# Two DeltaNet directions in one TensorE stream: the chunk inverse is issued between the state and output products of the step ahead, and the decays of the next step are formed early

## Chip, cores and metric

The kernel runs on one core of a Trainium2 chip. The metric is the device time of one execution in microseconds (us), the median of several runs. Times below are microseconds unless marked ns.

## The reference, cut to what matters

The program computes a two-layer backbone. One of the three branches of each layer is a gated DeltaNet, run forwards and backwards over a context prefix and the latent tokens, four heads of width 128, 512 tokens in all. What the change touches is this recurrence:

```python
decay = jnp.where(incl, jnp.exp(jnp.where(incl, diff, 0.0)), 0.0)
kb = k * beta[..., None]
m = jnp.where(strict, jnp.einsum('bhncd,bhnsd->bhncs', kb, k) * decay, 0.0)
t_inv = lax.linalg.triangular_solve(eye + m, jnp.broadcast_to(eye, m.shape), left_side=True, lower=True)
u = jnp.einsum('bhncs,bhnse->bhnce', t_inv, v * beta[..., None])
w = jnp.einsum('bhncs,bhnsd->bhncd', t_inv, kb * jnp.exp(gam)[..., None])
qk = jnp.einsum('bhncd,bhnsd->bhncs', q, k) * decay

def step(s, xs):
    q_c, k_c, u_c, w_c, qk_c, gam_c = xs
    v_new = u_c - jnp.einsum('bhcd,bhde->bhce', w_c, s)
    o = (jnp.einsum('bhcd,bhde->bhce', q_c * jnp.exp(gam_c)[..., None], s)
         + jnp.einsum('bhcs,bhse->bhce', qk_c, v_new))
    g_last = gam_c[..., -1]
    s = (s * jnp.exp(g_last)[..., None, None]
         + jnp.einsum('bhcd,bhce->bhde', k_c * jnp.exp(g_last[..., None] - gam_c)[..., None], v_new))
    return s, o
```

## The kernel before

The kernel takes chunks of 128 tokens, so each layer has four steps, `j` = 0 to 3. In a step both directions `d` = 0 and 1 work on a tile of tokens each (`ORDER`), with all four heads. Layer 0 writes outputs for all four tiles; the last layer has only two tiles of latent tokens (`nt` = 2), so its steps 0 and 1 write no outputs. All products are fp32 and go through the helper `mm` (L1576), whatever they compute. The order of work on each engine is the order of the code; engines are kept apart by counted semaphores.

A product of four heads, 128x128 by 128x128 each, is called a big group here: four calls, eight instructions in the trace. A product of eight 64x64 blocks (`by_block`) is a small group: eight calls, sixteen instructions in the trace.

A step before the change, on TensorE:

1. Head. `decay`: running sums of the log decay as a matrix, a big group for each direction into bank ONE. `kk` (K times K transposed) into bank TWO. `kq` (keys by queries) into ONE once the decays have been read. VectorE masks the decays (L2086) and ScalarE takes two exponentials of each (L1114 for E, L1115 for the gain EG). VectorE then makes, for one direction after the other, the chain L2095, L2096, L2098, L2100, L2103, L2106: the matrix of the inverse, its first level and its transpose `X`. GpSimd masks the levels (L786).
2. Levels n = 1 to 5 of the inverse, by doubling. For each level: first half of direction 0 and 1 (level times X into TWO), ScalarE copies the result to `Y` (L1127), second half of direction 0 and 1 (XT times Y into ONE), VectorE subtracts (L2114) and transposes (L2118). At the end `beside` and a corner product join the two halves of the 128x128 inverse `T_full`.
3. Tail. `w` (T times decayed keys) and its negated copy on ScalarE (L1142), `fresh` (T times values, and from step 1 on, minus w times state), scaled by beta on VectorE (L2134) into `vnew`, `outs` (state by gained queries from step 1 on, and vnew by scores), `state` (decayed keys by vnew), then the new state on VectorE (L2141, or L2145 from step 1 on). The next step's `decay` waits for the new state, since both use bank ONE.

Banks 0 to 3 hold products of the stages around the DeltaNet and stand free during it. Decayed keys `kg` and `kd` are made on ScalarE by four small scalings each (L1106).

## Time and profile before

| what | value |
|---|---|
| median of 3 runs | 2748.91 us (2747.64 to 2752.01) |
| the profiled execution, its own time | 2748.07 us |
| span of its trace, first to last instruction | 2746.3 us |
| mean granted TensorE clock | 0.963 of full speed |
| the four DeltaNet steps of layer 0 | 149.5 us |
| the four DeltaNet steps of layer 1 | 143.2 us |

The span is the time between the first and the last instruction; the metric has 1.8 us more around it. The two stage times are the sums of four windows each, which are shown below with the busy time of every engine. A busy TensorE is an upper bound on its work, because matmuls overlap and their ends are modelled.

### The profile page before, as it was taken

To read this page: it belongs to the slowest core of one execution; us is meant where nothing else is said; L and a number is where in the kernel's file an instruction comes from. 1 tells how busy PE (TensorE), PEld (TensorE's weight loads), DVE (VectorE), ACT (ScalarE), POOL (GpSimd) and SP (SyncE) were. 2 spreads that over 40 slices of the span, in tenths; PEclk is the share of its full clock that TensorE was granted. 3 is DMA by queue.
4 is the path that set the end of the run, shared out by engine and by line. 5 is a ranking of instruction groups with operands and counts; after the bars stand their busy time and mean duration, and the time that the engine had idled before them with its cause. 6 is when DMAs were issued, how large, how long until landed. Compare 5 with 4: busy or idle time off the path is not lost.

```text
span 2746.3 us, 38445 instructions
## 1 busy us (share of the span) xinstructions
PE 2550.2 (93%) x16316; PEld 2089.2 (76%) x16316; DVE 1346.9 (49%) x2118; ACT 1000.8 (36%) x1551; POOL 80.2 (3%) x108
## 2 busy tenths in 40 slices
PE   3999998989888899989999989999988968889999
PEld 2777776856678777767777768888875758889899
DVE  4323335357776643463332353333355676666654
ACT  2222212355653422232222132322245574344543
POOL 0000000000012100000000000000000002200000
PEclk6999999999989999999999999999999989999999
DMA  5444433201110033324444432222230210034454
GB/s 235 163 175 180 173 138 123 93 31 47 62 47 2 2 132 144 123 75 170 184 165 157 147 139 98 102 92 100 100 108 31 92 62 2 2 133 175 158 183 167
DMA packets 44664, 309.66 MB, mean 113 GB/s; under 512 B 5072, under 2 KB 6224, under 8 KB 7632
## 3 DMA queue, kind: packets, MB, share of 16 engines
q1 hardware_dynamic: 44208, 305.95, 30.3%
q8 instruction: 130, 2.13, 0.3%
q10 hardware_dynamic: 288, 1.27, 0.1%
q14 instruction: 38, 0.31, 0.0%
HBM read 306.15 MB, written 1.05 MB: 112 GB/s over the span
## 4 chain that ended last, share of the span: by engine, by line
PE 85%; DVE 8%; ACT 3%; issue 2%; DMA 1%; SPq 0%; ACTq 0%; DVEq 0%
PE bank L1287 68%; PE bank L1576 7%; PE bank L1303 2%; PE bank L1280 2%; DVE rt L1715 2%; PE bank L1522 1%; PE bank L1500 1%; DVE w_lo L1704 1%; DMA ring<-in_wts 1%; ACT L830 1%; PE bank L1509 1%; ACT w_hi L812 1%; DVE u_lo L1744 1%; DVE sq L1754 0%; DVE work L2103 0%
## 5 line engine op out<-in xcount | busy, mean ns | idle before, releaser
L1704 DVE TENSOR_TENSOR w_lo<-ring,w_hi 128x1024 fp32r<-128x1024 f32 x420 | 510.8, 1224 | 1048.5 <-ACT w_hi L812 1045.5
L1287 PE MATMUL bank<-u_hi,w_hi 128*128 128x512 f32 (+1 forms) x2208 | 817.1, 370 | 84.0 <-DVE w_lo L1704 46.7
L1287 PE MATMUL bank<-u_hi,w_lo 128*128 128x512 f32 (+1 forms) x2208 | 801.6, 363 | 0.0
L1287 PE MATMUL bank<-u_lo,w_hi 128*128 128x512 f32 (+1 forms) x2208 | 799.3, 362 | 0.0
L812 ACT ACTIVATE w_hi<-ring 128x1024 fp32r<-128x1024 f32 x420 | 441.2, 1058 | 965.1 <-PE bank L1287 657.9
L1287 PEld LDWEIGHTS bank<-u_hi,w_hi 128*128 128x128 f32 x2208 | 422.8, 191 | 180.6 <-issue 83.6
L1287 PEld LDWEIGHTS bank<-u_lo,w_hi 128*128 128x128 f32 x2208 | 422.5, 191 | 64.7
L1287 PEld LDWEIGHTS bank<-u_hi,w_lo 128*128 128x128 f32 x2208 | 423.0, 192 | 63.8 <-issue 3.4
L1576 PE MATMUL bank<-work 64*64 64x64 f32 (+1 forms) x3952 | 233.5, 246 | 38.1 <-DVE work L2106 21.4
L1287 PE MATMUL bank<-hidden_hi,w_hi 128*128 128x512 f32 (+1 forms) x704 | 259.8, 369 | 0.0
L1576 PEld LDWEIGHTS bank<-work 64*64 64x64 f32 (+1 forms) x3952 | 220.8, 159 | 50.4 <-POOL work L786 31.8
L1287 PE MATMUL bank<-hidden_hi,w_lo 128*128 128x512 f32 (+1 forms) x704 | 258.5, 367 | 0.0
L1287 PE MATMUL bank<-hidden_lo,w_hi 128*128 128x512 f32 (+1 forms) x704 | 258.5, 367 | 0.0
L1287 PEld LDWEIGHTS bank<-hidden_hi,w_hi 128*128 128x128 f32 x704 | 132.5, 188 | 28.6 <-issue 4.9
L1287 PEld LDWEIGHTS bank<-hidden_lo,w_hi 128*128 128x128 f32 x704 | 132.5, 188 | 24.3
L1287 PEld LDWEIGHTS bank<-hidden_hi,w_lo 128*128 128x128 f32 x704 | 132.5, 188 | 23.7
L1715 DVE RECIPROCAL rt<-rt 128x512 f32<-128x512 f32 (+1 forms) x30 | 92.5, 3082 | 43.1 <-ACT rt L830 43.1
L1303 PE MATMUL bank<-ring,cond 128*32 128x256 f32 x1152 | 82.9, 408 | 21.4 <-DMA ring<-in_wts 21.4
L864 ACT ACTIVATE hidden_hi<-sg 128x512 fp32r<-128x512 f32 (+1 forms) x88 | 50.7, 579 | 127.9 <-DVE sg L1810 127.9
L871 ACT ACTIVATE sg<-bank 128x512 f32<-128x512 f32 (+1 forms) x88 | 46.7, 535 | 116.4 <-PE bank L1287 116.3
L786 POOL TENSOR_TENSOR work<-work,cst 128x256 f32<-128x256 f32 x80 | 67.9, 867 | 417.7 <-DVE work L2098 398.5
L1303 PEld LDWEIGHTS bank<-ring,cond 128*32 128x32 f32 x1152 | 31.4, 114 | 64.0 <-issue 32.1
(195 smaller groups left out, 2407.9 us busy)
## 6 DMA issues: line engine op xcount, KB each, us to landing
ring<-in_wts SPq DMA_DIRECT2D x288, 1024.0 KB, 4.9
h<-in_x SPq DMA_DIRECT2D x8, 256.0 KB, 10.5
par<-in_par ACTq DMA_DIRECT2D x2, 620.0 KB, 6.0
out<-h SPq DMA_DIRECT2D x8, 128.0 KB, 4.1
cst<-in_cst SPq DMA_DIRECT2D x1, 672.0 KB, 10.1
mod_par<-in_mod SPq DMA_DIRECT2D x1, 96.0 KB, 9.7
cond<-in_c SPq DMA_DIRECT2D x1, 8.0 KB, 1.6
```

Of the source, the lines that this page charges most:

```text
L786: pool.tensor_tensor(level[:, d, n % 2, :, :], mt[:, d, :, :], mask, ALU.mult).then_inc(level_ready[d], 1)
L812: act.activation(w_hi[:, b % HALVES, :], half_source(n % RING, part), ACT.Copy).then_inc(weights_rounded, 1)
L830: act.activation(rt[rows, n % 2, 0:w], bank[4 + n % 2][rows, 0:w], ACT.Sqrt, bias=eps[rows, :], scale=1.0 / size).then_inc(roots, 1)
L864: act.activation(h_hi[:, 2 * i + c, 0:w], sg[:, c, 0:w], ACT.Copy).then_inc(hidden_rounded, 1)
L871: act.activation(sg[:, c, 0:w], bank[(q0 + c) % 4][:, 0:w], ACT.Silu).then_inc(drained["a"], 1)
L1280: last = weights.used(pe.matmul(out, lhsT, rhs, start=n == 0, stop=n == len(parts) - 1))
L1287: last = weights.used(pe.matmul(out, lhs[a], rhs[b], start=start and n == 0, stop=stop and n == 2))
L1303: last = pe.matmul(bank[7 - unit % 2][32 * j:32 * j + 32, 0:256], cond32[:, k, :], panel[:, kk, j, :], start=k == 0, stop=k == DC - 1)
L1500: pe.matmul(bank[S_BANKS[a % 4]][:, 0:keys.stop - keys.start], qq[0:QK, hd, t * P:(t + 1) * P], kk[0:QK, hd, keys], start=True, stop=True) ...
L1576: return pe.matmul(out, lhsT, rhs, start=start, stop=stop)
L1704: tt(w_lo[:, b % HALVES, :], half_source(n % RING, part), w_hi[:, b % HALVES, :].bitcast(F32), ALU.subtract).then_inc(panel_left[n % RING] ...
L1715: step(dve.reciprocal(r, r))
```

## The change

Three things change inside the DeltaNet stage.

The algebra: `w` and its negated copy are gone, and so is w times state. In their place `keyed` multiplies the tile's keys by the state (a big group for each direction, steps 1 to 3), and VectorE forms V = values minus decayed `keyed` (`keyed_values`). `fresh` is then a single product T times V, and ScalarE scales it by beta into V in four small scalings (`fresh_values`), where VectorE did it in one operation.

The banks: decays, keys by queries, fresh values and outputs use banks 0 and 2 (FRESH); state and keyed use banks 1 and 3 (STATE). The inverse keeps ONE and TWO.

The order: step j's inverse is issued together with the fresh values, state and outputs of step j-1. `outs` stand in level 1, `key_query` in level 2, `keyed` in level 3, and the decays of step j+1 behind level 5. Gained queries (L2182 of the changed kernel), scores (L2186) and `keyed_values` (L2167) stand behind levels 2, 3 and 4 on VectorE, the new state behind levels 1 and 2. The decayed keys are made on ScalarE behind levels 3 and 4. `beside` has one buffer for both directions, and gained queries go to `rt`.

```diff
-        kg = view(24, 2)
-        blocks = view(26, 5).rearrange("p n (d h c) -> p n d h c", d=2, h=HEADS)
-        mt, beside, X, XT, Y = [blocks[:, n, :, :, :] for n in range(5)]
+        kd = view(24, 2)
+        blocks = view(26, 4).rearrange("p n (d h c) -> p n d h c", d=2, h=HEADS)
+        mt, X, XT, Y = [blocks[:, n, :, :, :] for n in range(4)]
+        V = view(30, 2)
         level = view(32, 2).rearrange("p d (n h c) -> p d n h c", n=2, h=HEADS)
         T_full = view(34, 2)
-        vnew, kd, nwT = E, kg, view(32, 2)
+
+        beside = ada_turned[:, :].rearrange("p (h c) -> p h c", h=HEADS)
+        gain_q = rt
...
+        FRESH, STATE = [bank[0], bank[2]], [bank[1], bank[3]]
...
+                def keep_output(d, j):
+                    t = ORDER[d][j]
+                    if j >= 0 and j % 2 == 0 and t < nt:
+                        act.wait_ge(out_made[d], outs_before(l, j, d) + 1)
+                        act.activation(yb[:, :, t * P:(t + 1) * P], heads(FRESH[d][:, :]), ACT.Copy).then_inc(out_kept[d], 1)
+
+                def decay_keys(d, j):
+                    if j < 3:
+                        act.wait_ge(state_made[d], 3 * l + j)
+                        t = ORDER[d][j]
+                        scaled_heads(kd[:, d, :], ktok[:, t, :], kds[:, d, t, :]).then_inc(kd_ready[d], 1)
+
...
+                def decays(j):
+                    for d in range(2):
+                        act.wait_ge(decay_masked[d], l * 4 + j + 1)
+                        act.activation(E[:, d, :], E[:, d, :], ACT.Exp).then_inc(decay_exp[d], 1)
+                        act.wait_ge(gain_ready[d], l * 4 + j)
+                        act.activation(EG[:, d, :], FRESH[d][:, :], ACT.Exp).then_inc(gain_exp[d], 1)
+
+                def fresh_values(d, j):
+                    act.wait_ge(fresh_made[d], l * 4 + j + 1)
+                    scaled_heads(V[:, d, :], FRESH[d], beta[:, ORDER[d][j], 4 * d:4 * d + 4]).then_inc(fresh_ready[d], 1)
+
+                decays(0)
...
+                    if j:
+                        for d in range(2):
+                            fresh_values(d, j - 1)
...
+                        if n == 1:
+                            for d in range(2):
+                                keep_output(d, j - 1)
+                        if n > 2 and n < 5:
+                            decay_keys(n - 3, j)
...
-                    for d in range(2):
-                        act.wait_ge(w_made[d], it + 1)
-                        act.activation(nwT[:, d, :], TWO[d][:, :], ACT.Copy, scale=-1.0).then_inc(w_kept[d], 1)
...
-
+                        decays(j + 1)
+                for d in range(2):
+                    fresh_values(d, 3)
...
+                def decay(d, j):
+
+                    t = ORDER[d][j]
+                    if j:
+                        pe.wait_ge(kq_read[d], l * 4 + j)
+                    elif d == 0:
+                        wait_drained(pe, (l, "z", 3))
+                    upto = C("upto" if d == 0 else "from")
+                    each(lambda hd, c, _: mm(FRESH[d][:, c], g[:, t, 4 * d + hd:4 * d + hd + 1].to_broadcast([P, P]),
+                                             upto), d, j).then_inc(decay_made[d], 1)
+
+                def fresh(d, j):
+
+                    pe.wait_ge(t_ready[d], l * 4 + j + 1)
+                    pe.wait_ge(kq_read[d], l * 4 + j + 1)
+                    if j < 3:
+                        pe.wait_ge(decay_masked[d], l * 4 + j + 2)
+                        pe.wait_ge(gain_exp[d], l * 4 + j + 2)
+                    if j:
+                        pe.wait_ge(keyed_ready[d], 3 * l + j)
+                    t = ORDER[d][j]
+                    each(lambda hd, c, _: mm(FRESH[d][:, c], T_full[:, d, c], V[:, d, c] if j else vtok[:, t, c]),
+                         d, j).then_inc(fresh_made[d], 1)
+
+                def state(d, j):
+                    pe.wait_ge(fresh_ready[d], l * 4 + j + 1)
+                    pe.wait_ge(kd_ready[d], 3 * l + j + 1)
+                    each(lambda hd, c, _: mm(STATE[d][:, c], kd[:, d, c], V[:, d, c]), d, j).then_inc(state_made[d], 1)
+
+                def outs(d, j):
+                    if ORDER[d][j] < nt:
+                        pe.wait_ge(fresh_ready[d], l * 4 + j + 1)
+                        pe.wait_ge(gain_ready[d], l * 4 + j + 1)
+
+                        def head_out(hd, c, _):
+                            if j:
+                                mm(FRESH[d][:, c], S[:, d, c], gain_q[:, d, c], stop=False)
+                            return mm(FRESH[d][:, c], V[:, d, c], att[:, d, c], start=j == 0)
+                        each(head_out, d, j).then_inc(out_made[d], 1)
+
+                def keyed(d, j):
+
+                    pe.wait_ge(state_ready[d], 3 * l + j)
+                    each(lambda hd, c, t: mm(STATE[d][:, c], kT[:, hd, t], S[:, d, c]), d, j).then_inc(keyed_made[d], 1)
+
+                def key_query(d, j):
+                    if j:
+                        pe.wait_ge(fresh_ready[d], l * 4 + j)
+                        pe.wait_ge(out_kept[d], outs_before(l, j, d))
+                    else:
+                        pe.wait_ge(decay_masked[d], l * 4 + 1)
+                        pe.wait_ge(gain_exp[d], l * 4 + 1)
+                    each(lambda hd, c, t: mm(FRESH[d][:, c], kT[:, hd, t], qT[:, hd, t]), d, j).then_inc(kq_made[d], 1)
+
+                for d in range(2):
+                    decay(d, 0)
...
+                    def beside_level(n, d):
+
+                        if n == 1 and j:
+                            outs(d, j - 1)
+                        elif n == 2:
+                            key_query(d, j)
+                        elif n == 3 and j:
+                            keyed(d, j)
...
+                        if it:
+                            pe.wait_ge(y_kept[d], it * LEVELS)
+                        each(lambda hd, c, t: mm(TWO[d][:, c], kT[:, hd, t], kT[:, hd, t]), d, j).then_inc(kk_made[d], 1)
+                    if j:
+                        for d in range(2):
+                            fresh(d, j - 1)
...
+                            if n == 1 and j:
+                                state(d, j - 1)
+                            first_half(n, d)
+                        beside_level(n, 0)
...
+                            second_half(n, d)
+                        beside_level(n, 1)
+                    if j < 3:
+                        for d in range(2):
+                            decay(d, j + 1)
...
-                    for d in range(2):
-                        pe.wait_ge(kg_ready[d], it + 1)
-                        pe.wait_ge(t_ready[d], it + 1)
-                        each(lambda hd, c, t: mm(TWO[d][:, c], kg[:, d, c], T_full[:, d, c]), d).then_inc(w_made[d], 1)
...
+                for d in range(2):
+                    fresh(d, 3)
+                for d in range(2):
+                    outs(d, 3)
...
+                def new_state(d, j):
+                    dve.wait_ge(state_made[d], 3 * l + j + 1)
+                    dve.wait_ge(out_made[d], outs_before(l, j + 1, d))
+                    if j == 0:
+                        dve.tensor_copy(S[:, d, :], STATE[d][:, :]).then_inc(state_ready[d], 1)
+                    else:
+                        for hd in range(HEADS):
+                            c = slice(hd * P, (hd + 1) * P)
+                            last = stt(S[:, d, c], S[:, d, c], eL[:, d, ORDER[d][j], hd:hd + 1], STATE[d][:, c],
+                                       ALU.mult, ALU.add)
+                        last.then_inc(state_ready[d], 1)
+
+                def keyed_values(d, j):
+                    dve.wait_ge(keyed_made[d], 3 * l + j)
+                    t = ORDER[d][j]
+                    for hd in range(HEADS):
+                        c = slice(hd * P, (hd + 1) * P)
+                        last = stt(V[:, d, c], STATE[d][:, c], egam[:, d, t, hd:hd + 1], vtok[:, t, c], ALU.mult, ALU.add)
+                    last.then_inc(keyed_ready[d], 1)
+
+                def add_output(d, j):
+                    t = ORDER[d][j]
+                    if j % 2 and t < nt:
+                        out = yb[:, :, t * P:(t + 1) * P]
+                        dve.wait_ge(out_made[d], outs_before(l, j, d) + 1)
+                        dve.wait_ge(out_kept[1 - d], outs_before(l, j, 1 - d))
+                        tt(out, out, heads(FRESH[d][:, :]), ALU.add).then_inc(out_kept[d], 1)
+
+                def gained_queries(d, j):
+                    t = ORDER[d][j]
+                    dve.wait_ge(gain_exp[d], l * 4 + j + 1)
+                    dve.wait_ge(out_made[d], outs_before(l, j, d))
+                    tt(heads(gain_q[:, d, :]), heads(EG[:, d, :]), qT[:, :, t * P:(t + 1) * P], ALU.mult).then_inc(gain_ready[d], 1)
+
+                def scores(d, j):
+                    dve.wait_ge(kq_made[d], l * 4 + j + 1)
+                    tt(att[:, d, :], FRESH[d][:, :], E[:, d, :], ALU.mult).then_inc(kq_read[d], 1)
+
+                def decays(j):
+                    for d in range(2):
+                        dve.wait_ge(decay_made[d], l * 4 + j + 1)
+                        for hd in range(HEADS):
+                            c = slice(hd * P, (hd + 1) * P)
+                            last = stt(E[:, d, c], FRESH[d][:, c], gam[:, d, ORDER[d][j], hd:hd + 1],
+                                       C("not_upto" if d == 0 else "not_from"), ALU.subtract, ALU.min)
+                        last.then_inc(decay_masked[d], 1)
+
+                decays(0)
...
+                    if j == 0:
+                        dve.wait_ge(factors_ready, l + 1)
...
+                        if n == 1 and j:
+                            for d in range(2):
+                                add_output(d, j - 1)
+                            new_state(0, j - 1)
+                        elif n == 2:
+                            if j:
+                                new_state(1, j - 1)
+                            for d in range(2):
+                                gained_queries(d, j)
+                        elif n == 3:
+                            for d in range(2):
+                                scores(d, j)
+                        elif n == 4 and j:
+                            for d in range(2):
+                                keyed_values(d, j)
+                    if j < 3:
+                        decays(j + 1)
+                for d in range(2):
+                    add_output(d, 3)
```

TensorE, step 1 of layer 0, before: the rows from its decays to those of step 2. "cst,small" is the decay product; "work 64x64" the inverse, with `beside` and the corners; the 48 behind it are w, fresh, outs and state, and the 16 ahead of it kk and kq.

```order
L1576 MATMUL bank<-cst,small 128x128 x8
L1576 MATMUL bank<-work 128x128 x16
L1576 MATMUL bank<-work 64x64 x192
L1576 MATMUL bank<-work 128x128 x48
L1576 MATMUL bank<-cst,small 128x128 x8
```

TensorE, the same place in the changed kernel: from the decays of step 1, which now stand in step 0, to `keyed` of the first direction in level 3. The row of 20 is kk, fresh of step 0, and its state for direction 0.

```order
L1594 MATMUL bank<-cst,small 128x128 x8
L1594 MATMUL bank<-work,ada_turned 64x64 x8
L1594 MATMUL bank<-work 64x64 x8
L1594 MATMUL bank<-work 128x128 x20
L1594 MATMUL bank<-work 64x64 x8
L1594 MATMUL bank<-work 128x128 x4
L1594 MATMUL bank<-work 64x64 x8
L1594 MATMUL bank<-work 128x128 x4
L1594 MATMUL bank<-work 64x64 x16
L1594 MATMUL bank<-work 128x128 x4
L1594 MATMUL bank<-work 64x64 x16
L1594 MATMUL bank<-work 128x128 x4
```

The inverse was one run of 192 block products; now big groups of four stand between its halves, and no product waits for a new state ahead of kk.

VectorE, the end of step 0 and the head of step 1 before: fresh values, new state, masked decays, then the chain for direction 0.

```order
L2134 TENSOR_TENSOR work<-bank,small 128x512 x2
L2141 COPY work<-bank 128x512 x2
L2086 SCALAR_TENSOR_TENSOR work<-bank,small,cst 128x128 x8
L2095 TENSOR_TENSOR work<-bank,work 64x256 x2
L2096 TENSOR_TENSOR work<-bank,work 64x256
L2098 TENSOR_TENSOR work<-work,small 128x256
L2100 TENSOR_TENSOR work<-work,cst 128x256
L2103 TENSOR_TENSOR work<-cst,work 128x256
L2106 STREAM_TRANSPOSE work<-work 128x256
```

VectorE in levels 1 to 3 of step 1 in the changed kernel: each pair of rows is the subtraction and the transpose of one direction.

```order
L2225 TENSOR_TENSOR work<-work,bank 128x256
L2229 STREAM_TRANSPOSE work<-work 128x256
L2154 COPY work<-bank 128x512
L2225 TENSOR_TENSOR work<-work,bank 128x256
L2229 STREAM_TRANSPOSE work<-work 128x256
L2225 TENSOR_TENSOR work<-work,bank 128x256
L2229 STREAM_TRANSPOSE work<-work 128x256
L2154 COPY work<-bank 128x512
L2182 TENSOR_TENSOR rt<-work 128x512 x2
L2225 TENSOR_TENSOR work<-work,bank 128x256
L2229 STREAM_TRANSPOSE work<-work 128x256
L2225 TENSOR_TENSOR work<-work,bank 128x256
L2229 STREAM_TRANSPOSE work<-work 128x256
L2186 TENSOR_TENSOR work<-bank,work 128x512 x2
```

The copies to the new state, the gained queries (rt) and the scores (128x512 x2 from the bank) moved in between the subtractions, which the next products of the inverse wait for.

## Rows read from the trace of the kernel before

**Rows 1.** The page of the profile: busy engines, and the chain that ended last by line.

```profile
PE 2550.2 (93%) x16316; PEld 2089.2 (76%) x16316; DVE 1346.9 (49%) x2118; ACT 1000.8 (36%) x1551; POOL 80.2 (3%) x108
...
PE bank L1287 68%; PE bank L1576 7%; PE bank L1303 2%; PE bank L1280 2%; DVE rt L1715 2%; PE bank L1522 1%; PE bank L1500 1%; DVE w_lo L1704 1%; DMA ring<-in_wts 1%; ACT L830 1%; PE bank L1509 1%; ACT w_hi L812 1%; DVE u_lo L1744 1%; DVE sq L1754 0%; DVE work L2103 0%
```

**Rows 2.** Busy time in eight steps: window, us, engines' busy (instructions), PEclk, DMA share, GB/s.

```profile
793.70:829.40 35.70, 31.02 (x496) 29.47 (x497) 22.68 (x51) 16.29 (x42) 9.67 (x12) 0.89 0.01 2
829.40:866.70 37.30, 32.60 (x530) 31.09 (x529) 23.80 (x55) 13.38 (x36) 9.72 (x12) 0.95 0.01 2
866.70:906.10 39.40, 33.89 (x530) 32.14 (x530) 24.87 (x60) 14.55 (x38) 9.70 (x12) 0.91 0.01 2
906.10:943.20 37.10, 31.22 (x515) 29.40 (x513) 24.01 (x56) 11.11 (x28) 9.70 (x12) 0.95 0.01 2
2262.30:2297.20 34.90, 30.09 (x480) 28.47 (x481) 22.30 (x51) 15.14 (x40) 9.69 (x12) 0.85 0.01 2
2297.20:2331.40 34.20, 29.39 (x498) 27.57 (x496) 23.79 (x56) 13.38 (x36) 9.72 (x12) 0.95 0.01 2
2331.40:2368.80 37.40, 32.72 (x529) 31.09 (x530) 24.01 (x58) 14.56 (x38) 9.71 (x12) 0.95 0.01 2
2368.80:2405.50 36.70, 30.91 (x514) 29.03 (x512) 24.30 (x56) 11.12 (x28) 9.68 (x12) 0.95 0.01 2
```

**Rows 3.** Timeline of the head of step 1, layer 0: start, us, engine, line, operation.

```profile
829.41 2.10 PE L1576 MATMUL bank<-cst,small 128*128 128x128 f32 x16
...
831.35 3.75 PE L1576 MATMUL bank<-work 128*128 128x128 f32 x32
831.66 0.63 ACT L1114 ACTIVATE work<-work 128x512 f32<-128x512 f32 x1 [2.35 <-DVE work L2086]
832.20 0.58 ACT L1115 ACTIVATE work<-bank 128x512 f32<-128x512 f32 x1
832.59 0.86 DVE L2095 TENSOR_TENSOR work<-bank,work 64x256 f32<-64x256 f32 x2
...
836.14 0.68 PE L1576 MATMUL bank<-work 64*64 64x64 f32 x16 [1.04 <-POOL work L786]
...
838.95 0.45 DVE L2106 STREAM_TRANSPOSE work<-work 128x256 f32<-128x256 f32 x1
839.43 1.29 DVE L2109 TENSOR_TENSOR work<-bank,work 128x512 f32<-128x512 f32 x2
...
839.50 2.79 PE L1576 MATMUL bank<-work 64*64 64x64 f32 x47 [2.68 <-DVE work L2106]
```

**Rows 4.** Timeline of about one level of the inverse in step 0, layer 0, ScalarE and VectorE.

```profile
811.71 0.38 ACT L1127 ACTIVATE work<-bank 128x256 f32<-128x256 f32 x1 [1.37 <-PE bank L1576]
...
812.03 0.99 DVE L2130 TENSOR_TENSOR work<-work 128x512 f32<-128x512 f32 x1
...
812.96 0.42 DVE L2114 TENSOR_TENSOR work<-work,bank 128x256 f32<-128x256 f32 x1
...
813.79 0.38 DVE L2114 TENSOR_TENSOR work<-work,bank 128x256 f32<-128x256 f32 x1
...
814.25 0.39 ACT L1127 ACTIVATE work<-bank 128x256 f32<-128x256 f32 x1 [1.37 <-PE bank L1576]
```

**Rows 5.** Timeline of the end of step 1, layer 0.

```profile
854.15 12.76 PE L1576 MATMUL bank<-work 64*64 64x64 f32 x120 [0.57 <-DVE work L2114]
...
855.97 0.38 ACT L1137 ACTIVATE work<-bank 64x256 f32<-64x256 f32 x1 [0.30 <-PE bank L1576]
...
858.45 2.43 ACT L1106 ACTIVATE work<-work,small 128x128 f32<-128x128 f32 x8
...
866.95 1.12 DVE L2145 SCALAR_TENSOR_TENSOR work<-work,small,bank 128x128 f32<-128x128 f32 x4 [1.56 <-PE bank L1576]
```

**Rows 6.** A window of 2 us where the levels of step 1 begin.

```profile
840.00:842.00 2.00, 2.00 (x43) 2.00 (x41) 1.17 (x4) 0.38 (x1) 1.55 (x3) 0.50 0.04 8
```

**Rows 7.** Window behind the last step of layer 0.

```profile
943.20:1000.00 56.80, 51.90 (x228) 39.52 (x229) 36.06 (x23) 24.19 (x27) 0.00 (x0) 0.94 0.25 95
```

183 lines of the change are left out of this document (48 added, 135 removed).

## The prediction

> **What bounds the kernel now.** I read the page first. TensorE is busy 93% of the span and leads the chain that ended last; L1576, the helper of the DeltaNet, holds 7% of that chain [rows 1]. So the stage is on the path, and only its own length matters. The windows by step give that length: 35.7 + 37.3 + 39.4 + 37.1 = 149.5 us in layer 0 and 34.9 + 34.2 + 37.4 + 36.7 = 143.2 us in layer 1, 292.7 us in all. VectorE is busy 23 to 25 of some 37 us in a step, ScalarE 11 to 16, GpSimd 10 [rows 2].
>
> The timeline then shows three regimes within a step.
>
> Head: 16 decay instructions start at 829.41, kk and kq follow (32 instructions in 3.75 us, so a big group takes 0.94), then TensorE waits 1.04 us, does one small group, and waits 2.68 us more for VectorE's chain of the second direction [rows 3]. The chain is 838.95 + 0.45 - 832.59 = 6.8 us for both directions, 3.4 each. From the first decay to the second direction's first block product: 839.50 - 829.41 = 10.1 us.
>
> Levels: a level repeats every 814.25 - 811.71 = 2.54 us. The reader should see that this is a latency loop: product, copy to Y 0.38, product, subtraction 0.42, with about 0.2 from a product's end to its reader. From the start of the subtraction at 813.79 to that of the copy at 814.25 one small group has ended behind another: 0.46 [rows 4]. Four of them are 1.9 us, so TensorE is short of work for 0.65 us in a level, though the trace calls it busy.
>
> Tail: from 854.15 TensorE runs 120 instructions in 12.76 us without a gap. The last corner is copied at 855.97, so it ended 0.2 earlier, near 855.8; the rest, 96 instructions of w, fresh, outs and state, lasts until 866.7 [rows 2, 5]. There TensorE is the bound.
>
> **The change, part by part.** I lay out one step of the changed kernel with those durations and count from the start of kk. A big group is 0.94, a small one 0.47.
>
> *Removed work.* w costs 8 big groups per layer and w times state 6; keyed adds 6. So 8 big groups per layer go, 2 x 8 x 0.94 = 15 us. That is the part that needs no overlap. The copies to the negated w were hidden behind fresh.
>
> *New head.* kk 0 to 1.9. Corner copies on ScalarE end at 0.6, then E of direction 0 until 1.23 (0.63) and its EG until 1.8 (0.58), direction 1 until 3.0 [rows 3]. VectorE's decays for this step were issued behind level 5 and end near 1.3. The chain then runs 1.3 to 8.1. Beside it TensorE issues fresh: 1.9 to 2.9 and 3.1 to 4.1. ScalarE scales four times 128x128 out of PSUM. No row of before shows this form; the nearest are 2.43 / 8 = 0.30 from SBUF [rows 5], and 0.58 for four times that width from PSUM [rows 3], so 0.15 and 0.58 each are the ends. I take 0.30, the same shape: 1.2 us per direction, done at 4.3 and 5.5. At 0.15 each layer's end is 1.2 us shorter; at 0.58 the scalings end at 7.7, each of six heads is 0.5 longer and each end 2.2, 7.4 us in all. State 4.4 to 5.3, a small group to 5.8, state to 6.6, then TensorE waits for the chain and starts the second direction's block product at 8.25. That wait of 1.7 us stands for the 3.7 us of before; 8.25 stands for 10.1, with fresh and state inside it.
>
> The Trainium skill (VectorE: DVE Perf Modes, the section on the TRN2 errata) gives a ScalarE operation from PSUM 172 + 128 cycles at 1.2 GHz, an estimate of 0.25 us. By it a direction's scaling takes 1.0 instead of 1.2, which shortens the end of each layer by 0.4 us at most. No row here shows it.
>
> *Levels.* Level 1 now holds four small and four big groups (outs): it ends at 13.45, 5.2 us. Level 2 with kq is 4 x 0.47 + 2 x 0.94 = 3.75. Level 3 with keyed the same, but VectorE is late there: two subtractions with transposes 1.75, new state 1.12 [rows 5], gained queries 2 x 0.99 [rows 4] are 4.9 us, and the loop loses 0.4. Behind level 3 the scores, 1.29 us [rows 3], and behind level 4 keyed values, 8 of the 0.28 us operations, 2.24 us [rows 5], stretch levels 4 and 5 to 3.0 and 3.2. Decays of the next step 1.85 on TensorE; they cover part of VectorE's lateness. Beside and corners 1.85. Sum: 5.2 + 3.75 + 4.2 + 3.0 + 3.2 + 1.85 + 1.85 = 23.05, and a step is 8.25 + 23.05 = 31.3 us. Without outs (layer 1, steps 1 and 2) it is 28.1: the level gets 3.75 shorter but back to its latency loop, which returns 0.5. Step 3 has no decays behind it: 30.3. Before, these steps were 34.2 to 39.4.
>
> *Step 0.* Before, up to its last corner: 35.7 less a tail of eight big groups, 7.5, is 28.2 us; layer 1 has no outs there and gives 34.9 less six groups (5.6) and a wait for the scaled fresh values that I put at 1 (an operation of 0.6 to 0.7 and its signals), also 28. Its head stays. Two kq groups move into level 2 (+1.3 beyond the slack), VectorE's gained queries and scores come together (+1.4), decays of step 1 come behind (+1.0): 31.9.
>
> *End.* Behind the last corner: fresh 0.3 to 2.1, scalings to 3.8, outs to 6.45, addition: 6.65 us, where nothing covers ScalarE's scaling. This is what that edit costs, some 0.5 us per direction and layer more than one operation of 512 columns, which takes 0.6 to 0.7 [rows 3].
>
> *Sum.* Layer 0: 31.9 + 31.3 + 31.3 + 30.3 + 6.65 = 131.4. Layer 1: 31.9 + 28.1 + 28.1 + 30.3 + 6.65 = 125.1. Together 256.5 against 292.7: minus 36.2. Layouts by hand leave out small waits: between every two dependent products the trace has up to 0.1 more than I counted, so I give back 0.4 per step, 3.2 in all. That leaves minus 33.0. The profiled execution was 2748.1, which gives 2715.1; the median stands 0.8 above it, so 2716.
>
> *Waits.* A wait that is added is fresh on decays of the same step having been read (bank FRESH). Queued behind it are state and the second direction's first block product; I have it satisfied at 1.8 and 3.0, 6 us before the chain ends, so it costs nothing while VectorE's chain is the later of the two. DMAs are not moved; the stage has a DMA share of 0.01 [rows 2].
>
> **Rivals.**
>
> *The clock dips as before.* Where the levels begin, the granted clock was 0.50 (1.2 GHz) after the waits of the head [rows 6], and the steps average 0.85 to 0.95 [rows 2]. My layout counts steps 1 to 3 at 2.4 GHz, as the waits shrink from 3.7 to 1.7 us. If the clock falls all the same, it now falls on outs, which is TensorE's own work: 2 us of half clock cost 1 us, four cost 2. Six steps at 1 to 2 us give back 6 to 12: 2722 to 2728. For it: four or five short waits in a head and new ones in levels 3 to 5. Against: in the levels of before, which wait too, the product pace stays at 2.54. The Trainium skill warns of this (TensorE: Matmul & The Clock Gate, on psum-queue depth-cycling): short idles between groups that cycle through banks let the clock oscillate. By that rule this rival would hold; the 2.54 us loop does not bear it out.
>
> *No overlap.* The order on TensorE is fixed, so each inserted group can make the next one late on ScalarE or VectorE. If the slack of the levels and of the head is used up by these, only the removed products stay: minus 15, 2734. For it: VectorE gets 5 us of work in level 2 where it had 2.7. Against: it is busy only 23 to 25 us in a step [rows 2], and keeps about that.
>
> *Slower.* One mechanism: TensorE never stays long enough at work in a step, and runs the whole step at 1.2 GHz. Its 29 us of work then take some 55, about 20 us more than my 31.3 plus waits. With two of eight steps like this the gain of 33 is gone; with four the time is near 2760. The clock of 0.85 in step 0 of layer 1 shows it is possible for a part of a step, no row shows it for a whole one.
>
> *No change.* The stage gets shorter but the stage behind waits, for instance for weights: 2749. There TensorE is busy 51.9 of 56.8 us and DMA at a quarter of its share [rows 7], so nothing there is late.
>
> **How the numbers follow.** Likeliest case, a stage 26 to 42 us shorter: 0.68. The clock rival 0.15, no overlap 0.10, slower 0.03, no change 0.04. The lower end of the range takes away my allowance of 3.2 and VectorE's lateness (0.4 + 0.5 in six steps, half of it): 2749 - 36 - 3, and 3 for what the layout misses the other way, the cheap end of the scalings among it, 2707. The upper end takes in the clock rival and touches the case of no overlap: 2732. A measurement of this kernel tells 0.2%, 5.5 us, from no change. Faster 0.94, same 0.03, slower 0.03.
>
> **What would show it.** L1142 and L2134 are gone. The steps, from one group of decay products to the next, take about 31 us, and 28 in layer 1 where no outs are. TensorE's longest wait in a step stands ahead of the second direction's first block product, released by VectorE's chain, at 1.5 to 2 us. Level 2 is 3.8 us or a little more. The granted clock is above 0.95 in steps 1 to 3. The prediction is wrong if TensorE waits for GpSimd's masks or for ScalarE in the head, if levels 4 and 5 take over 4 us because VectorE is behind, or if the clock falls in outs.

## The result, and the profile after

The changed kernel takes 2718.4 us (median; the kernel before in the same session 2748.7). The ratio is 0.9886, 95% interval 0.9867 to 0.9905: 31 us, or 1.1%, faster. One execution of the changed kernel was disturbed (3219 us) and is left out of the comparison. The profiled execution took 2717.1 with a span of 2715.3, so the span is 31.0 shorter than before.

The page of the changed kernel, its busy engines and its chain, as [rows 1]:

```profile
PE 2537.8 (93%) x16188; PEld 2067.7 (76%) x16188; DVE 1345.8 (50%) x2150; ACT 990.6 (36%) x1537; POOL 79.7 (3%) x108
...
PE bank L1308 69%; PE bank L1594 6%; PE bank L1324 2%; PE bank L1301 2%; DVE rt L1784 2%; PE bank L1543 1%; PE bank L1521 1%; DVE w_lo L1773 1%; DMA ring<-in_wts 1%; ACT L834 1%; PE bank L1530 1%; ACT w_hi L816 1%; DVE u_lo L1813 1%; DVE sq L1823 0%; DVE work L2207 0%
```

L1594 is the helper that was L1576. Its share of the chain fell from 7 to 6%, TensorE lost 128 instructions and 12.4 us of busy time. The chain is otherwise the same, so the gain was made in the DeltaNet stage. The windows by step answer to [rows 2]; here each begins with the decays of its step, and the fourth window of a layer holds step 3 and the end:

```profile
794.50:822.40 27.90, 22.39 (x401) 20.81 (x401) 18.29 (x45) 10.18 (x27) 9.44 (x12) 0.79 0.01 2
822.40:852.90 30.50, 28.78 (x498) 26.36 (x496) 22.79 (x57) 13.29 (x36) 9.86 (x12) 1.00 0.01 3
852.90:885.30 32.40, 30.79 (x517) 28.17 (x513) 25.77 (x67) 12.10 (x34) 9.59 (x12) 1.00 0.01 2
885.30:928.00 42.70, 39.05 (x594) 35.74 (x592) 27.93 (x72) 14.67 (x41) 9.58 (x12) 1.00 0.01 2
2246.20:2274.70 28.50, 22.45 (x401) 20.98 (x401) 18.18 (x45) 10.18 (x27) 9.43 (x12) 0.82 0.01 3
2274.70:2303.50 28.80, 26.96 (x484) 24.60 (x481) 22.89 (x57) 12.09 (x34) 9.90 (x12) 1.00 0.01 2
2303.50:2332.20 28.70, 26.98 (x482) 24.54 (x480) 24.37 (x65) 12.09 (x34) 9.63 (x12) 1.00 0.01 2
2332.20:2375.20 43.00, 39.09 (x596) 35.75 (x592) 27.99 (x72) 14.92 (x41) 9.60 (x12) 1.00 0.01 2
```

Layer 0 takes 133.5 us (149.5 before), layer 1 129.0 (143.2): 30.2 less together. Two columns are to be read. TensorE's busy time in step 1 of layer 0 is 28.8 of 30.5, so the step ends close to its work. And the granted clock is 1.00 in all of steps 1 to 3, where it was 0.91 to 0.95; in step 0, whose waits stay, it is 0.79 and 0.82.

The timeline of step 1 of layer 0 answers to [rows 3] and [rows 5]:

```profile
822.38 2.05 PE L1594 MATMUL bank<-cst,small 128*128 128x128 f32 x16
...
827.76 0.88 DVE L2207 TENSOR_TENSOR work<-bank,work 64x256 f32<-64x256 f32 x2 [1.61 <-PE bank L1594]
...
829.59 2.18 ACT L1110 ACTIVATE work<-bank,small 128x128 f32<-128x128 f32 x8 [0.30 <-PE bank L1594]
...
830.79 2.86 PE L1594 MATMUL bank<-work 128*128 128x128 f32 x32 [0.23 <-ACT work L1110]
...
834.14 0.45 DVE L2218 STREAM_TRANSPOSE work<-work 128x256 f32<-128x256 f32 x1
...
834.68 18.33 PE L1594 MATMUL bank<-work 64*64 64x64 f32 x384 [1.04 <-POOL work L790]
...
837.11 0.42 DVE L2225 TENSOR_TENSOR work<-work,bank 128x256 f32<-128x256 f32 x1 [2.53 <-PE bank L1594]
...
841.45 0.42 DVE L2225 TENSOR_TENSOR work<-work,bank 128x256 f32<-128x256 f32 x1 [2.07 <-PE bank L1594]
...
843.63 1.81 DVE L2182 TENSOR_TENSOR rt<-work 128x512 f32<-128x512 f32 x2
...
845.78 0.42 DVE L2225 TENSOR_TENSOR work<-work,bank 128x256 f32<-128x256 f32 x1 [0.33 <-PE bank L1594]
...
849.11 0.42 DVE L2225 TENSOR_TENSOR work<-work,bank 128x256 f32<-128x256 f32 x1 [0.47 <-PE bank L1594]
...
850.72 2.12 DVE L2167 SCALAR_TENSOR_TENSOR work<-bank,small,work 128x128 f32<-128x128 f32 x8
...
852.76 0.41 DVE L2225 TENSOR_TENSOR work<-work,bank 128x256 f32<-128x256 f32 x1
```

Head: TensorE's long row of 384 instructions begins at 834.68, with the second direction's first block product, behind a wait of 1.04. The row of 48 that starts at 825.51 (one of the rows left out) holds the corners, kk and fresh; in its single records kk begins at 826.52, so the head takes 8.2 us with fresh, state and the first small group inside it. The row puts the wait down to GpSimd's masks, but the mask that this product needs had ended at 833.82, and VectorE's transpose of that direction ended at 834.14 + 0.45 = 834.59, 0.09 ahead of the start: the chain is what comes last. It ran from 827.76, 6.8 us, as before. ScalarE's eight scalings from PSUM take 2.18, 0.27 us each. Levels: the subtractions of direction 0 start at 837.11, 841.45, 845.78, 849.11 and 852.76, 3.3 to 4.3 us apart, against 2.5 before, with outs, kq and keyed on TensorE and VectorE's new pieces between them. The last subtraction has no idle time ahead of it: VectorE comes straight from the keyed values (850.72 + 2.12).

Four windows of the changed kernel: the first 2 us of levels as [rows 6], level 2 and level 3 of the same step by TensorE's first product in each, and the stage behind as [rows 7]:

```profile
834.60:836.60 2.00, 1.92 (x30) 1.76 (x32) 0.00 (x0) 0.49 (x2) 2.00 (x4) 1.00 0.04 8
838.55:842.88 4.33, 4.33 (x81) 3.96 (x80) 2.19 (x6) 1.37 (x3) 1.42 (x2) 1.00 0.02 4
842.88:847.22 4.34, 4.34 (x82) 3.96 (x81) 3.94 (x8) 1.93 (x6) 3.22 (x4) 1.00 0.02 4
928.00:984.80 56.80, 51.96 (x230) 39.56 (x231) 36.51 (x24) 24.13 (x27) 0.00 (x0) 0.94 0.26 97
```

Where the clock was 0.50 it is now 1.00. Levels 2 and 3 hold the same products, four small and two big groups, and take the same 4.33 us, although VectorE is busy for 2.19 us in one and 3.94 in the other: there TensorE's own products set the pace. The stage behind has the same 52.0 busy in 56.8 us: nothing was given back there.

### The profile page after: what moved, and what is told of

It is laid out like the page before. It is cut to its first block, busy times and chain, and to the rows that moved or that the text cites. A ratio compares the mean times of both kernels' runs of the same rounds, so it can differ in the third digit from the quotient of the medians.

```text
span 2715.3 us, 38257 instructions
## 1 busy us (share of the span) xinstructions
PE 2537.8 (93%) x16188; PEld 2067.7 (76%) x16188; DVE 1345.8 (50%) x2150; ACT 990.6 (36%) x1537; POOL 79.7 (3%) x108
## 4 chain that ended last, share of the span: by engine, by line
PE 85%; DVE 8%; ACT 4%; issue 2%; DMA 1%; POOL 0%; SPq 0%; DVEq 0%; ACTq 0%
PE bank L1308 69%; PE bank L1594 6%; PE bank L1324 2%; PE bank L1301 2%; DVE rt L1784 2%; PE bank L1543 1%; PE bank L1521 1%; DVE w_lo L1773 1%; DMA ring<-in_wts 1%; ACT L834 1%; PE bank L1530 1%; ACT w_hi L816 1%; DVE u_lo L1813 1%; DVE sq L1823 0%; DVE work L2207 0%
## 5 line engine op out<-in xcount | busy, mean ns | idle before, releaser
L1594 PE MATMUL bank<-work 64*64 64x64 f32 (+1 forms) x3616 | 205.8, 237 | 21.7 <-DVE work L2218 10.5
L1594 PEld LDWEIGHTS bank<-work 64*64 64x64 f32 (+1 forms) x3616 | 185.8, 149 | 38.5 <-POOL work L790 17.8
L1879 DVE TENSOR_TENSOR sg<-sg,bank 128x512 f32<-128x512 f32 (+1 forms) x88 | 54.1, 618 | 58.0 <-PE bank L1308 57.9
L1324 PEld LDWEIGHTS bank<-ring,cond 128*32 128x32 f32 x1152 | 31.4, 114 | 63.4 <-issue 32.1
## 6 DMA issues: line engine op xcount, KB each, us to landing
h<-in_x SPq DMA_DIRECT2D x8, 256.0 KB, 10.7
```

The source lines that it names most:

```text
L1324: last = pe.matmul(bank[7 - unit % 2][32 * j:32 * j + 32, 0:256], cond32[:, k, :], panel[:, kk, j, :], start=k == 0, stop=k == DC - 1)
L1594: return pe.matmul(out, lhsT, rhs, start=start, stop=stop)
L1879: tt(sg[:, c, 0:w], sg[:, c, 0:w], bank[(q0 + 2 + c) % 4][:, 0:w], ALU.mult).then_inc(drained["v"], 1)
```

## The experiments

Differences are against the changed kernel, if nothing else is said. Each time is the median, with that of the kernel before in the same session in brackets. The fences show the lines of an edit on which the argument hangs; the matching lines on the other engines are left out.

**The algebra without the order (xa_algebra_only).** Fresh, outs and state go back behind the inverse, decays and kq into the head; keyed products in place of w stay.

```diff
-                    if j < 3:
-                        for d in range(2):
-                            decay(d, j + 1)
+                    for d in range(2):
+                        fresh(d, j)
+                    for d in range(2):
+                        outs(d, j)
+                        if j < 3:
+                            state(d, j)
```

> This kernel keeps the new algebra, the new banks and the scaling on ScalarE, but puts the work back in the order of before: decays, kk and kq in the head of their own step, and fresh, outs and state behind the corners of their own step (keyed stays in level 3). My theory, that the removed products are worth 15 us and the rest comes from filling TensorE's waits and from the clock: 2749 less 13 to 19, so about 2733. The rival that the removed work and the removed copy explain nearly all of the gain: 2720 or less. The rival that the removed products are cancelled by the uncovered scaling on ScalarE: 2745 or more.

Measured 2747.07 (2749.33), ratio 0.9993 [0.9983, 1.0002]. The theory missed: the saved 15 us of products did not appear, and the rival of 2745 or more held. The kernel was not a clean test, though. Its outputs stayed in bank FRESH, which the next decays need, so the decays waited for VectorE's addition of outputs, and gained queries and scores stood in the levels. The next kernel takes both away.

**The algebra with everything else in its old place (xa2_algebra_only_old_places).** Outputs go to bank TWO, as before; VectorE makes the scores in the head, behind the chains, and one gained query behind each of levels 1 and 2. The edit, against the changed kernel, also holds that of xa; only the lines on the bank are shown.

```diff
-                                mm(FRESH[d][:, c], S[:, d, c], gain_q[:, d, c], stop=False)
-                            return mm(FRESH[d][:, c], V[:, d, c], att[:, d, c], start=j == 0)
+                                mm(TWO[d][:, c], S[:, d, c], gain_q[:, d, c], stop=False)
+                            return mm(TWO[d][:, c], V[:, d, c], att[:, d, c], start=j == 0)
```

> The new algebra in the order of before, more closely than the first such kernel: the scores are formed in the head behind the chains and the gained queries one per level, outputs use the inverse's second bank as before, so that the decays need not wait for an output to be copied. keyed and keyed values stay behind levels 3 and 4, the scaling on ScalarE. My theory now, that the removed products are worth something near 15 us but keyed values (2.1 us on VectorE in a loop of latencies, six times) and the uncovered scaling take about half back: 2735 to 2740. The rival that the algebra is worth its 15 us and the first kernel lost them by its scores and waits: 2730 to 2734. The other rival, that the algebra alone is worth nothing wherever the rest stands: 2745 or more.

Measured 2746.22 (2750.12), 0.9987 [0.9978, 0.9996]: 3.6 us faster than before, between 1.1 and 6.0. The theory of 2735 to 2740 missed; the rival that the algebra alone is worth nothing (2745 or more) held. Its timeline of step 1, layer 0:

```profile
826.45 2.10 PE L1590 MATMUL bank<-cst,small 128*128 128x128 f32 x16
...
836.54 15.81 PE L1590 MATMUL bank<-work 64*64 64x64 f32 x352 [2.67 <-DVE work L2203]
...
855.69 0.38 ACT L1165 ACTIVATE work<-bank 64x256 f32<-64x256 f32 x1 [0.30 <-PE bank L1590]
856.78 2.17 ACT L1110 ACTIVATE work<-bank,small 128x128 f32<-128x128 f32 x8 [0.71 <-PE bank L1590]
...
857.98 0.49 PE L1590 MATMUL bank<-rt,work 128*128 128x128 f32 x2 [0.34 <-ACT work L1110]
...
863.44 1.06 PE L1590 MATMUL bank<-cst,small 128*128 128x128 f32 x8
```

From decays to decays 37.0 us (37.3 before). The head is 836.54 - 826.45 = 10.1, as before [rows 3]. From there to the copy of the last corner it is 19.15, before 16.5 [rows 3, 5]: 2.7 more. Two keyed groups are 1.9 of that, and some 0.8 is lateness. From there to the next decays it is 7.75, before about 10.7 (to 866.7): 3.0 less, of which the four groups that are gone would be 3.75, so 0.75 was added, a wait of 0.34 for the scaling included (outs start at 857.98). So keyed, 2.7 us in a level, costs more than w times state did in the tail, 1.9, and most of what w itself saves goes to that and to the open scaling. Step 0, which has no keyed, is 1.3 us shorter (826.45 less 792.15, where its decays begin, 34.3).

By layer this kernel is 3.6 us shorter in layer 0 (145.9 for 149.5) and 1.6 longer in layer 1 (144.8 for 143.2). Windows of steps 1 and 2 of layer 1, and of 4 us in the tail of its step 1:

```profile
2290.50:2326.80 36.30, 31.12 (x483) 29.05 (x482) 24.05 (x62) 12.10 (x34) 9.70 (x12) 0.86 0.01 2
2326.80:2365.50 38.70, 33.74 (x512) 32.04 (x513) 24.35 (x64) 13.34 (x36) 9.68 (x12) 0.87 0.01 2
2318.00:2322.00 4.00, 4.00 (x33) 3.75 (x34) 0.53 (x2) 1.13 (x3) 0.00 (x0) 0.63 0.00 0
```

These steps take 36.3 and 38.7 us where they took 34.2 and 37.4 [rows 2], at a granted clock of 0.86 and 0.87 where it was 0.95: in step 1, which has no outs, TensorE comes to its tail of four groups at 0.63. By the clocks alone this is at most some 3 us in each of the two steps (0.09 of 36), if all of a step went by the clock. Without it the algebra would have been worth 9 or 10 us at most, still not 15; that is an estimate and was not run.

**Decays late (x2_late_decays).** Only the next step's decays return to the head of their own step.

```diff
+                    if j:
+                        for d in range(2):
+                            decay(d, j)
...
-                    if j < 3:
-                        for d in range(2):
-                            decay(d, j + 1)
```

> The changed kernel with one move undone: the decay products of a step are issued on TensorE ahead of its kk instead of behind level 5 of the step ahead. My theory: kk and VectorE's chain start about 2 us later and the end of the levels gives back 1, so 1 to 2 us in each of six steps: 2725 to 2730. The rival that the early decays only moved work, since TensorE has to do it anyway: 2717 to 2720.

Measured 2729.65 (2749.33), 0.9931 [0.9916, 0.9946], as expected: some 11 us of the gain hang on this one move. Most steps are only 1.2 us longer. But in the head of step 2, layer 0:

```profile
855.54 0.65 PE L1594 MATMUL bank<-work,ada_turned 64*64 64x64 f32 x8 [0.57 <-DVE work L2225]
...
857.26 3.44 PE L1594 MATMUL bank<-cst,small 128*128 128x128 f32 x16
...
859.03 1.13 DVE L2193 SCALAR_TENSOR_TENSOR work<-bank,small,cst 128x128 f32<-128x128 f32 x4 [2.87 <-PE bank L1594]
...
861.87 0.87 DVE L2207 TENSOR_TENSOR work<-bank,work 64x256 f32<-64x256 f32 x2
```

The same 16 decay instructions take 3.44 us in place of 2.05, and the chain begins 4.6 us behind the first of them. The windows ahead of them and over them show the clock:

```profile
855.00:856.00 1.00, 0.46 (x8) 0.49 (x9) 0.99 (x3) 0.38 (x1) 0.00 (x0) 1.00 0.00 0
856.00:857.20 1.20, 1.20 (x20) 1.05 (x17) 0.16 (x1) 0.75 (x2) 0.00 (x0) 1.00 0.00 0
857.30:860.70 3.40, 3.40 (x18) 3.40 (x18) 1.13 (x4) 0.89 (x2) 0.00 (x0) 0.55 0.00 0
```

It fell from 1.00 to 0.55, mostly its lower level of 1.2 GHz; TensorE had been busy for 0.46 of a microsecond and then all of the 1.2 us ahead of the fall. Part of that microsecond is a wait of 0.57 for VectorE's last subtraction, a place that the decays fill in the changed kernel. That step takes 35.1 against 32.35, so 1.6 us more than the 1.2 of the others. The clock fell once more over the decays of step 3 of layer 0, but over none of the decays of steps 1 to 3 in layer 1. From the first decay to the last product, layer 0 became 5.7 us longer and layer 1 3.1. The moved decays thus cost some 1 us a step by their length, and more where the clock falls over them; that the waits ahead bring the fall is likely, but the same waits stand in layer 1 without it.

**Fresh values on VectorE (x4_fresh_on_vector).** One operation of 512 columns per direction, between the chains of the two directions, in place of ScalarE's four scalings.

```diff
+                        if j and d == 0:
+                            for e in range(2):
+                                fresh_values(e, j - 1)
```

> The changed kernel with one part undone: the fresh values are scaled by beta in one VectorE operation per direction, placed between the chains of the two directions. My theory: the second chain, which the second direction's first block product waits for, starts 1.3 us later in six steps, and each of the two ends gets 0.5 us shorter: 7 us slower than the changed kernel, 2725. The rival that ScalarE's four scalings are themselves on the path (state waits for them): as fast as the changed kernel or faster, 2718 or less.

Measured 2724.02 (2749.33), 0.991 [0.9895, 0.9925], as expected. TensorE's decay rows give the steps:

```profile
822.08 2.05 PE L1589 MATMUL bank<-cst,small 128*128 128x128 f32 x16
...
853.82 2.05 PE L1589 MATMUL bank<-cst,small 128*128 128x128 f32 x16
...
887.35 2.05 PE L1589 MATMUL bank<-cst,small 128*128 128x128 f32 x16
```

31.74 and 33.53 us, each 1.2 longer than with ScalarE: the two operations stand inside the chain that the head waits for. At the end of a layer they are shorter than the scalings, which gives back 0.5.

**The kernel before with the clock held up (x5_before_filled).** To price the clock alone, the kernel before gets three groups of products into the idle bank 0 where the levels begin. They are extra work whose results nothing reads.

```diff
+                            if n == 1:
+                                for _ in range(d + 1):
+                                    each(lambda hd, c, t: mm(bank[0][:, c], kT[:, hd, t], kT[:, hd, t]), d)
```

> The kernel before, with products of no use (three big groups per step, into a free bank that nobody reads) in the two waits of each head, so that TensorE is at work there. Everything else waits as before. It measures what the clock alone was worth. My theory: the granted clock of steps 1 to 3 goes from 0.91 to 0.95 up to 1.00, and the steps get 1 to 2 us shorter each: 2737 to 2742. The rival that the clock cost nothing because the levels are a loop of latencies: 2749, or a little more for the added products.

Measured 2743.39 (2749.33), 0.9979 [0.9969, 0.9988]: 6 us faster, 3 to 9, a little less than the expected 7 to 12 and clear of the rival that the clock cost nothing. Windows of steps 1 and 2, layer 0:

```profile
830.90:867.50 36.60, 34.66 (x555) 32.71 (x554) 23.56 (x55) 13.36 (x36) 9.67 (x12) 1.00 0.01 2
867.50:905.40 37.90, 35.10 (x554) 32.83 (x554) 25.08 (x60) 14.54 (x38) 9.66 (x12) 1.00 0.01 2
```

Granted clock 1.00, where it was 0.95 and 0.91, and 36.6 and 37.9 us where it was 37.3 and 39.4 [rows 2], although each step has 24 instructions more. So the clock is worth some 6 us to the kernel before, with the price of the added products taken off. How much of the changed kernel's 31 us is the clock's was not measured by itself.

**Outs in the head (x1_outs_in_head).** The outs of direction 0 fill the wait ahead of the second direction's first block product.

```diff
-                            outs(d, j - 1)
+                            if d == 1:
+                                outs(1, j - 1)
...
+                                if d == 1:
+                                    outs(0, j - 1)
```

> The changed kernel with outs of direction 0 moved from behind the first halves of level 1 to ahead of the second direction's first block product, where TensorE waits about 1 us for VectorE's chain. My theory, that this wait is the one that bounds the head: 1 us less in the four steps that follow a step with outs (less 0.9 for the one in layer 0 whose outs are half as long), so 3 to 4 us faster than the changed kernel: 2715. The rival that level 1 is bound by its latencies and only the place of the wait changes: 2718, within 1 us.

Measured 2714.34 (2749.68), 0.9867 [0.9851, 0.9884], as expected. The decay rows:

```profile
823.66 2.05 PE L1594 MATMUL bank<-cst,small 128*128 128x128 f32 x16
...
853.21 2.05 PE L1594 MATMUL bank<-cst,small 128*128 128x128 f32 x16
...
884.45 2.05 PE L1594 MATMUL bank<-cst,small 128*128 128x128 f32 x16
```

Steps of 29.55 and 31.24, 1.0 and 1.1 shorter: the last wait of the head was real idle time, worth its 1.0 us.

**First scores in the head (x6_first_scores_in_head).** In step 0 kq goes from level 2 into the head, where TensorE waits for the chain and has nothing else.

```diff
-                        elif n == 2:
+                        elif n == 2 and j:
                             key_query(d, j)
...
+                    else:
+                        for d in range(2):
+                            key_query(d, 0)
```

> The changed kernel with keys by queries of step 0 issued right behind kk, as before the change, where TensorE waits 2.7 us. Steps 1 to 3 are untouched. My theory: level 2 of step 0 loses 1.3 us per layer, and the clock rises earlier (the changed kernel has 0.79 and 0.82 in step 0, where the kernel before had 0.89 and 0.85), worth 1 us more per layer: 4 to 5 us faster than the changed kernel: 2714. The rival that step 0 is bound by VectorE, which gets no less work: within 1 us of 2718.

Measured 2717.04 (2749.68), 0.9882 [0.9867, 0.9896]. Missed: step 0 became 26.9 and 27.5 us, only 1.0 shorter in each layer. The rival, that step 0 is bound by VectorE, held. The timeline of its levels tells why:

```profile
812.10 2.13 DVE L2185 TENSOR_TENSOR rt<-work 128x512 f32<-128x512 f32 x2
...
814.15 0.41 DVE L2228 TENSOR_TENSOR work<-work,bank 128x256 f32<-128x256 f32 x1
...
814.71 6.10 PE L1594 MATMUL bank<-work 64*64 64x64 f32 x160 [1.03 <-DVE work L2228]
...
820.74 2.05 PE L1594 MATMUL bank<-cst,small 128*128 128x128 f32 x16
```

VectorE makes the gained queries of both directions (2.13 us) and only then the subtraction of level 3, for which TensorE now waits 1.03. TensorE lost two groups of work there, VectorE did not.

**Both (xb_both).** x1 and x6 together.

```diff
-                            outs(d, j - 1)
-                        elif n == 2:
+                            if d == 1:
+                                outs(1, j - 1)
+                        elif n == 2 and j:
```

> Both moves together: outs of direction 0 ahead of the second direction's first block product, and keys by queries of step 0 in its head. They touch different steps, so by my theory the gains add up: 7 to 9 us faster than the changed kernel, 2710. The rival that neither wait bounds anything: 2718.

Measured 2714.28 (2749.68), 0.987 [0.9856, 0.9885]; the expected 2710 was missed by the same step 0 (27.0 us).

**VectorE's pieces spread (xc_spread_vector).** xb, and in step 0 one gained query or one scores operation behind each level instead of two.

```diff
+                        if j == 0:
+                            if n < 3:
+                                gained_queries(n - 1, j)
+                            elif n < 5:
+                                scores(n - 3, j)
```

> The kernel with both moves (outs of direction 0 and the first scores in the head), and in step 0 the gained queries and the scores are formed one per level on VectorE, behind levels 1 to 4, instead of two behind level 2 and two behind level 3. My theory, from the trace of the kernel with the first scores in the head, where TensorE waits 1.0 us behind the two gained queries: 1 to 1.5 us less per layer, 2711 to 2712. The rival that another latency bounds step 0: 2714.

Measured 2709.87 (2750.12), 0.9854 [0.9841, 0.9868], slightly better than expected. Step 0 takes 25.6 us (27.9 in the changed kernel) and 26.2 (28.5); steps 1 and 2 of layer 0 keep what x1 gave, 29.5 and 31.2. This version beats both kernels: its span is 2708.1 against 2715.3.

**Keyed values spread too (xd_spread_keyed).** In steps 1 to 3 scores and keyed values of one direction each go behind levels 3, 4 and 5.

```diff
+                            scores(0, j)
+                        elif n == 4:
+                            scores(1, j)
+                            keyed_values(0, j)
+                        elif n == 5:
+                            keyed_values(1, j)
```

> The kernel with VectorE's work of step 0 spread, and now also that of steps 1 to 3: scores of direction 0 behind level 3, scores of direction 1 and keyed values of direction 0 behind level 4, keyed values of direction 1 behind level 5. It tests what the algebra costs: levels 4 and 5 took 3.3 and 3.7 us in the changed kernel, where the loop alone takes 2.54, with two scores and eight keyed-value operations ahead of the subtractions. My theory, that this lateness is the price of keyed values: 0.7 to 1 us less in each of six steps, 2704 to 2706. The rival that the work behind level 5 delays the masked decays and the next chain by as much: 2710.

Measured 2709.41 (2750.56), 0.9853 [0.9836, 0.9869]; the rival, no gain, held. Its timeline:

```profile
819.11 2.05 PE L1594 MATMUL bank<-cst,small 128*128 128x128 f32 x16
...
847.01 1.11 DVE L2173 SCALAR_TENSOR_TENSOR work<-bank,small,work 128x128 f32<-128x128 f32 x4
848.03 0.41 DVE L2231 TENSOR_TENSOR work<-work,bank 128x256 f32<-128x256 f32 x1
...
848.66 2.05 PE L1594 MATMUL bank<-cst,small 128*128 128x128 f32 x16
```

The last subtraction of direction 0 starts 28.92 behind the step's decays, 29.36 in xc, but the next decays start after 29.55, as in xc (29.54) and x1. VectorE's lateness behind level 4 was not what set the step. From the first products of both directions on, the trace shows no wait of TensorE above 0.2. In levels 2 and 3 its own products set the pace, as the windows of the changed kernel show; what sets it in levels 4 and 5 was not isolated.

**The changed kernel once more (changed_again),** unedited, in the session of xd.

> The changed kernel itself, unchanged, so that the other kernel of this call and the one before the change are compared with it on one chip: 2718, ratio 0.989.

Measured 2716.75 (2750.56), 0.988 [0.9865, 0.9895], near the expected 2718. In that session xd is 7 us faster than it.

## Why the prediction was right, and which step of it was not

*Size and mechanism.* The stage was to get 36.2 us shorter by the layout and 33.0 after the allowance; it got 30.2 shorter. The head (8.25 us forecast, 8.2 measured), the start of the chain behind kk (1.3; 1.2), its length (6.8; 6.8) and the scaling (1.2 us a direction; 1.09) stand close to their rows. The wait was 1.04 for 1.7, since the state products ended 7.1 us behind kk and not 6.6.

*Terms that were mis-sized.* The layout gave 31.3 us to every step with outs, but the outs of step 0, issued in step 1, have no state product: two big groups, not four. Its own durations give 29.4 for step 1. Measured: 30.6, and 32.4 for step 2 (31.3), 28.8 twice in layer 1 (28.1). Step 3 from kk to its last corner is 31.4 (30.3), the end 7.05 (6.65), where the last addition takes 0.69 and had been given 0.2. Together the stage is 6.0 us longer than the layout, of which the allowance of 3.2 took half. The miscount in step 1 was luck: it made the layout 1.9 us longer, and with the right count the stage would have missed it by 7.9.

Where in step 1, by the first product of each part in the single records: level 1 took 3.9 us (3.3 with two big groups), level 2 4.3 (3.75), level 3 4.3 (4.2), levels 4 and 5 together 5.7 (6.2), the decays 2.0 (1.85), beside and corners 2.15 (1.85), the head nothing. So the term that was too small is the product group itself where kinds alternate: a big group between small ones took 1.09 us, not 0.94, and a small group took 0.51 to 0.57, not 0.47. And level 3 came out near its forecast for another reason than the one given: no time was lost to VectorE there, since level 2 takes as long with 1.75 us less of VectorE's work. The lateness of VectorE that was put into level 4 (3.0) did not come either; it took 2.5.

*The step that failed* is "That is the part that needs no overlap", of the 15 us of removed products, and with it the price of 2734 for the rival without overlap. xa2 has the removed products and not the order, and gains 3.6 us. Counting products was wrong on the path: w stood where TensorE was the bound, but keyed came into a level, where its two groups cost 2.7 us, the scaling lay open, and the clock fell further in layer 1. The rest, 28 us, came only with the order. It was right in sum because the layout counted new places and not savings.

*Where the 28 us are from.* Late decays cost 11 (x2), fresh values inside VectorE's chain 6 (x4). The clock is worth 6 (x5), but that was measured on the kernel before, and x2 contains some of it. These numbers overlap and are not terms of one sum. What fresh, state and outs save by lying in the head and in level 1 was not run alone.

*Rivals.* The clock rival (0.15) did not happen: 1.00 in steps 1 to 3. But x2 shows it is near: with the decays moved, waits stand ahead of the corners, and one step lost 1.6 us to the clock. The rule of the Trainium skill that was weighed (TensorE: Matmul & The Clock Gate, on psum-queue depth-cycling) would have had the clock fall; with waits of 1.04 between groups in turned banks the trace does not agree. No step of the changed kernel ran whole at half clock, so the slower rival did not come near; its sum was off too, since four steps at 20 us more give some 2796 and not 2760. "No change" fell with the stage behind, 51.96 busy of 56.8 against 51.90.

*Waits.* fresh waited for nothing that was new: VectorE's chain stayed the later, as forecast. GpSimd's masks are named in the row, which by the prediction's own sign would count against it, but the mask in question ended 0.77 us ahead of VectorE's transpose. Two signs did not come as given: level 2 took 4.3 us where 3.8 or a little more was named, and the longest wait was 1.04 where 1.5 to 2 was. The others came: the steps, and the clock of 1.00.

## What to carry to other kernels

Price removed work where it stood, and the work that replaces it where it now stands: eight groups less on an engine that is busy 93% of the time gave 3.6 us, and issuing the rest inside the latency loop gave 28. Price a group of products by the rows of the place where it will stand: among groups of another kind a big group took 1.09 us, not the 0.94 of a run of its own kind. In such a loop count every engine's inserted pieces per iteration: taking two products out of a level gained 1 us, and 1.3 us more came only when VectorE's four pieces were spread over four levels. Look first for the wait that is left at the longest chain, and put work there that is already possible (x1: 4 us).

## What the hardware showed

The granted clock of a stretch did not depend on busy share alone. With waits of 1.04 and 2.68 us and one small group between, it was 0.50 where the levels began [rows 6]; with one wait of 1.04 behind 2.86 us of products it stayed 1.00. In x2 it fell to 0.55 over 16 decay instructions that had 1.20 us of full work right ahead of them, and again over the decays of step 3 of layer 0. In the changed kernel it did not fall there. These 16 instructions took 3.44 us mostly at the lower level and 2.05 at the upper. ScalarE's scaling of 128x128 out of PSUM took 0.27 us, less than 0.30 from SBUF. By the Trainium skill (VectorE: DVE Perf Modes, the section on the TRN2 errata) the PSUM form is 172 + 128 cycles, an estimate of 0.25 us, and the trace is 0.02 above.
